# Input norm by token rows and side chunks ahead of main chunks, in a two-block transformer kernel on one core

## What is computed

```
def rms_norm(x, g):
    y = xf * lax.rsqrt(jnp.mean(xf * xf, axis=-1, keepdims=True) + RMS_EPS)
    return y * g

sh1, sc1, ga1, sh2, sc2, ga2 = split(silu(c) @ w_mod + b_mod)      # w_mod: 2048 x 12288; the same for c_ctx
px = (rms_norm(x,   norm_mix) * (1 + sc1)  + sh1)  @ w_in           # w_in: 2048 x 5568
pc = (rms_norm(ctx, norm_mix) * (1 + csc1) + csh1) @ w_in
```

## Time and profile before

| | us |
|---|---|
| median of 3 runs | 3162.58 |
| runs | 3152.15 to 3166.52 |
| the profiled execution, its own time | 3181.49 |
| its span in the profile | 3179.7 |
| TensorE busy | 3075.1 (97%) |
| VectorE busy | 2103.9 (66%) |
| ScalarE busy | 1571.3 (49%) |
| mean granted TensorE clock | 0.99 of full |

### The profile page before, as it was taken

How to read it: one execution, slowest core, us unless ns; L and a number is a source line. 1 busy time by engine, 2 the same in 40 slices (tenths; PEclk the granted TensorE clock), 3 DMA queues, 4 the chain that set the end, 5 groups by cost and what they waited for, 6 DMA issues and landing times.

```text
span 3179.7 us, 62622 instructions
## 1 busy us (share of the span) xinstructions
PE 3075.1 (97%) x26931; PEld 2652.4 (83%) x26931; DVE 2103.9 (66%) x2893; ACT 1571.3 (49%) x2161; POOL 245.3 (8%) x307
## 2 busy tenths in 40 slices
PE   6799999999999998999999999999999999999998
PEld 4578888888888887888888888888878888888887
DVE  5776656767787867555555556679977565655554
ACT  5555545565665644444444434456644444444333
POOL 1000000023332310000000000013200000000000
PEclk9899999999999999999999999999999999999999
DMA  9667766820000034666666565665555666666663
GB/s 334 202 212 244 244 221 212 256 79 8 12 8 8 8 110 152 198 186 186 185 186 186 184 194 185 207 181 157 157 164 173 186 186 187 187 188 193 186 186 126
DMA packets 549246, 529.56 MB, mean 167 GB/s; under 512 B 16916, under 2 KB 545706, under 8 KB 548074
## 3 DMA queue, kind: packets, MB, share of 16 engines
q1 hardware_dynamic: 546074, 516.08, 52.4%
q0 software_dynamic: 2832, 9.45, 0.9%
q10 hardware_dynamic: 64, 0.02, 0.0%
HBM read 521.28 MB, written 4.19 MB: 165 GB/s over the span
## 4 chain that ended last, share of the span: by engine, by line
PE 86%; DVE 9%; ACT 2%; DMA 2%; issue 1%; POOL 0%; DVEq 0%; ACTq 0%; POOLq 0%
PE ps L1991 38%; PE ps L1992 19%; PE ps L2122 10%; DVE lo L1210 3%; PE ps L2001 2%; PE ps L2030 2%; PE ps L2002 2%; PE ps L2003 2%; PE ps L2031 2%; PE ps L2384 1%; PE ps L2145 1%; PE ps L2132 1%; PE ps L2130 1%; ACT hi L796 1%; PE ps L2385 1%
## 5 line engine op out<-in xcount | busy, mean ns | idle before, releaser
L1210 DVE TENSOR_TENSOR lo<-raw,hi 128x1024 fp32r<-128x1024 f32 x936 | 1137.3, 1234 | 659.7 <-ACT hi L796 656.2
L796 ACT ACTIVATE hi<-raw 128x1024 fp32r<-128x1024 f32 x936 | 972.2, 1055 | 830.8 <-PE ps L1992 591.9
L1991 PE MATMUL ps<-mov,hi 128*128 128x512 f32 x3680 | 1303.8, 399 | 5.9 <-DVE mov L1272 4.6
L1992 PE MATMUL ps<-mov,lo 128*128 128x256 f32 x3680 | 1032.9, 281 | 0.0
L1991 PEld LDWEIGHTS ps<-mov,hi 128*128 128x128 f32 x3680 | 692.0, 188 | 180.9 <-issue 6.3
L1992 PEld LDWEIGHTS ps<-mov,lo 128*128 128x128 f32 x3680 | 695.5, 189 | 0.1
L1991 PE MATMUL ps<-hid,hi 128*128 128x512 f32 x704 | 248.8, 399 | 0.0
L2030 PE MATMUL ps<-hi,c 128*32 128x256 f32 x768 | 190.6, 288 | 40.5 <-DVE lo L1210 40.0
L816 ACT ACTIVATE tmp<-ps 128x512 f32<-128x512 f32 x157 | 93.8, 597 | 268.3 <-PE ps L1992 261.8
L1992 PE MATMUL ps<-hid,lo 128*128 128x256 f32 x704 | 197.7, 281 | 0.0
L2031 PE MATMUL ps<-lo,c 128*32 128x256 f32 x768 | 187.2, 284 | 0.0
(11 more groups left out here) (362 smaller groups left out, 4151.5 us busy)
## 6 DMA issues: line engine op xcount, KB each, us to landing
raw<-in_w_in SPq DMA_DIRECT2D x184, 512.0 KB, 4.6
raw<-in_w_mod SPq DMA_DIRECT2D x160, 512.0 KB, 4.9
raw<-in_w_gate SPq DMA_DIRECT2D x88, 512.0 KB, 4.6
raw<-in_w_up SPq DMA_DIRECT2D x88, 512.0 KB, 4.4
raw<-in_w_down SPq DMA_DIRECT2D x88, 512.0 KB, 4.3
raw<-in_w_ffn_gate SPq DMA_DIRECT2D x88, 512.0 KB, 4.6
raw<-in_w_ffn_up SPq DMA_DIRECT2D x88, 512.0 KB, 4.5
raw<-in_w_ffn_down SPq DMA_DIRECT2D x88, 512.0 KB, 4.4
```

Source lines behind the costliest of these rows:

```text
L796: act.activation(hi[:, s, :, :], src, ACT.Copy).then_inc(hi_ready, 1)
L1210: dve.tensor_tensor(lo[:, s, :, :], raw_at(ph, i, j)[0], hi[:, s, :, :].bitcast(F32), ALU.subtract)\
L1991: pe.matmul(ps[:, b, :], hi[:, s, kk, w], moving(k, None), start=first, stop=False)
L1992: mm = pe.matmul(ps[:, b, 0:T], lo[:, s, kk, w], moving(k, 0), start=False, stop=last)
```

## The change

1. **Squares by rows.** ScalarE squares each row tile of 128x2048 in one instruction that also sums along the row: two tiles of `ctx` after pair 4 and two of `x` after pair 5. The products with ones go. 1/rms is made of 128x4 numbers, after pairs 5 and 6 (`row_norm`), and VectorE writes `diag`, four 128x128 diagonals of these factors.
2. **Turn and scale in one product.** In pairs 7 to 14 TensorE multiplies blocks of the row tiles with `diag` (eight products of 128 columns per pair), which both turns and norms them. ScalarE copies the result out with the gain as scale (`scaled_at_pair`, four copies per pair, eight in pair 14). VectorE's 32 instructions of `first_product` go. The plain transposes of `x` stay (it is kept for the residual), four per pair in pairs 3 to 10, into bank 7, and VectorE copies both blocks at once; those of `ctx` go.
3. **The groups.** `first_hi` and `first_lo` no longer run two groups ahead of in_kv; all eight run in its first trip, at the chunks in `GROUP_AT`. TensorE waits once for all 32 scaled blocks before in_kv.
4. **The list of in_kv.** Each group of four side chunks now comes ahead of its main chunk, in every pair of every trip.

```diff
@@ -76,10 +76,9 @@
             self.order = [(False, p, c) for cs in ((0, 2, 3), (1,)) for p in range(pairs) for c in cs]
         for p in range(pairs if name not in ("out", "out_2") else 0):
             for c in self.rows_order:
-                self.order.append((False, p, c))
                 per = SIDES.get(name, 0) // pairs
-                if c < per:
-                    self.order += [(True, per * p + c, e) for e in range(n)]
+                group = [(True, per * p + c, e) for e in range(n if c < per else 0)]
+                self.order += group + [(False, p, c)] if name == "in_kv" else [(False, p, c)] + group
         self.chunks = len(self.order)
 
     def chunk(self, i, j):
...
@@ -324,14 +327,20 @@
 
     LOWS0 = PH["in_lora"].p0 + 1
 
-    XHAT_AT = {12: range(0, 8), 13: range(8, 16), 14: range(16, 24)}
-    XHAT_LATE = {3: range(24, 28), 7: range(28, 32)}
-    GROUP_AT = {1: 2, 2: 3, 5: 4, 6: 5, 8: 6, 9: 7}
+    NORM0 = 7
+    GROUP_AT = {0: 0, 1: 1, 2: 2, 3: 3, 6: 4, 8: 5, 10: 6, 12: 7}
+
+    def normed_at(p):
+        return range(2 * (p - NORM0), 2 * (p - NORM0) + 2) if NORM0 <= p < NORM0 + KB // 2 else range(0)
+
+    def scaled_at_pair(p):
+        return range(2 * (p - NORM0 - 1), 2 * (p - NORM0 - 1) + (4 if p == NORM0 + KB // 2 - 1 else 2)) if NORM0 < p < NORM0 + KB // 2 else range(0)
 
     def first_operand(n):
         q = 1 - n % 2
         k = n // 2
-        return q, k, (xhat[:, ds(k, 1), :], ctxT[:, ds(k, 1), :])[q]
+        x = xhat[:, k:k + 1, :] if k < KB - 4 else xhat_last[:, k - KB + 4:k - KB + 5, :]
+        return q, k, (x, ctxT[:, k:k + 1, :])[q]
 
     v_chain, a_chain, g_chain = sem("v_chain"), sem("a_chain"), sem("g_chain")
 
...
@@ -852,14 +862,23 @@
                 if p == VEC_AT:
                     act.wait_ge(vec_turned, 1)
                     act.activation(vec[:, :, :], ps[:, 5, :].rearrange("p (a n) -> p a n", a=4), ACT.Copy).then_inc(vec_ready, 1)
-                for k in turned_at(p):
-                    act.wait_ge(turned, k + 1)
-                    act.activation(ctxT[:, k, :], ps[:, TURN[k % 4], 0:T], ACT.Copy).then_inc(ctx_out, 1)
-                    if k >= 2:
-                        act.wait_ge(sq_used, k - 1)
-                    act.activation(sq[:, k % 2, :], ps[:, TURN[k % 4], :], ACT.Square).then_inc(sq_ready, 1)
-                if p == TURN0 + KB // 2 + 1:
-                    sqrt_of_variance(0, 2 * T)
+                if p in (TURN0 + 1, TURN0 + 2):
+                    act.wait_ge(row_in, 32)
+                    for h in range(2):
+                        src, n = ((crow, xrow)[p - TURN0 - 1], 2 * (p - TURN0 - 1) + h)
+                        if n:
+                            act.wait_ge(row_squared, n)
+                        act.activation(junk[:, :], src[:, h, :], ACT.Square, accum_out=row_sum[:, n:n + 1]).then_inc(row_squared, 1)
+                if p == TURN0 + 3:
+                    act.wait_ge(row_chain, 1)
+                    act.activation(row_root[:, :], row_var[:, :], ACT.Abs_reciprocal_sqrt).then_inc(row_rooted, 1)
+                for k in scaled_at_pair(p):
+                    if k == 0:
+                        act.wait_ge(gain_ready, 2)
+                    act.wait_ge(normed_turned, k + 1)
+                    for n in (2 * k, 2 * k + 1):
+                        q, _, dest = first_operand(n)
+                        act.activation(dest, ps[:, TURN[k % 4], (1 - q) * T:(2 - q) * T], ACT.Copy, scale=gain[:, q, k:k + 1]).then_inc(nt_ready, 1)
             gemm(PH["mod"], turn)
 
             def first_hi(g):
...
@@ -868,12 +887,12 @@
                     act.wait_ge(nt_ready, n + 1)
                     act.activation(mov1[:, ds(k, 1), 0, 1 - q, :], src, ACT.Identity, bias=modcol(0, q, k)).then_inc(nhi_ready, 1)
 
-            act.wait_ge(mod_ready, 4)
-            for g in range(2):
-                first_hi(g)
-
             def first_groups(i, j):
+                if i == 0 and j == 0:
+                    act.wait_ge(mod_ready, 4)
                 if i == 0 and j in GROUP_AT:
+                    if GROUP_AT[j] >= 6:
+                        act.wait_ge(mov_ready, 4 * GROUP_AT[j])
                     first_hi(GROUP_AT[j])
 
             def shift_both(i, p):
...
@@ -1280,16 +1299,32 @@
                 split(PH["mod"], 0, j)
 
 
+            def row_norm():
+                v, r, y = row_var[:, :], row_root[:, :], row_rstd[:, :]
+                dve.wait_ge(row_rooted, 1)
+                dve.tensor_tensor(v, v, r, ALU.mult).then_inc(row_chain, 1)
+                dve.wait_ge(row_chain, 2)
+                dve.scalar_tensor_tensor(out=v, in0=v, scalar=-0.5, in1=r, op0=ALU.mult, op1=ALU.mult).then_inc(row_chain, 1)
+                dve.wait_ge(row_chain, 3)
+                dve.scalar_tensor_tensor(out=y, in0=v, scalar=1.5, in1=r, op0=ALU.add, op1=ALU.mult).then_inc(row_chain, 1)
+                dve.wait_ge(row_chain, 4)
+                dve.tensor_tensor(diag[:, :, :], ident.rearrange("p (a n) -> p a n", a=1).broadcast_to([P, 4, P]),
+                                  y.rearrange("p (a n) -> p a n", n=1).broadcast_to([P, 4, P]), ALU.mult).then_inc(diag_ready, 1)
+
             def mod_row(i, p):
                 ph = PH["mod"]
                 part, n = 1 - p // 8, p % 8
                 dve.wait_ge(split_free, ph.last_chunk(i, p) + (1 + SPLIT_CREDIT))
                 dve.tensor_copy(mrow[:, n * CN:(n + 1) * CN], ps[0:4, ph.bank(p), 0:CN]).then_inc(bank_free, 1)
                 for k in turned_at(p):
-                    dve.wait_ge(sq_ready, k + 1)
-                    dve.tensor_copy(xT[:, k, :], ps[:, TURN[k % 4], T:2 * T]).then_inc(x_out, 1)
-                if p == TURN0 + KB // 2 + 1:
-                    variance(0, 2 * T)
+                    if k % 2 == 0:
+                        dve.wait_ge(turned, k // 2 + 1)
+                        dve.tensor_copy(xT[:, k:k + 2, :], ps[:, 7, :].rearrange("p (a t) -> p a t", a=2)).then_inc(x_out, 1)
+                if p == TURN0 + 2:
+                    dve.wait_ge(row_squared, 4)
+                    dve.tensor_scalar(row_var[:, :], row_sum[:, :], 1.0 / D, RMS_EPS, ALU.mult, ALU.add).then_inc(row_chain, 1)
+                if p == TURN0 + 3:
+                    row_norm()
                 if n == 7:
                     dve.wait_ge(vec_ready, 1)
                     dve.wait_ge(mcol_ready, p // 8 + 1)
...
@@ -1326,16 +1349,12 @@
                                              in1=mov1[:, ds(k, 1), 0, 1 - q, :].bitcast(F32), op0=ALU.add, op1=ALU.subtract).then_inc(mov_ready, 1)
 
             gemm(PH["mod"], mod_row)
-            dve.wait_ge(mod_ready, 4)
-            for g in range(2):
-                first_lo(g)
 
             def first_groups(i, j):
-                if i == 0:
-                    for item in XHAT_LATE.get(j, ()):
-                        first_product(item)
-                    if j in GROUP_AT:
-                        first_lo(GROUP_AT[j])
+                if i == 0 and j == 0:
+                    dve.wait_ge(mod_ready, 4)
+                if i == 0 and j in GROUP_AT:
+                    first_lo(GROUP_AT[j])
 
             def mod_row2(ph, i, m):
                 dve.wait_ge(split_free, ph.last_chunk(i, m, True) + (1 + SPLIT_CREDIT))
...
@@ -2039,19 +2058,22 @@
                     mm.then_inc(vec_turned, 1)
                 if p == TURN0:
                     pe.wait_ge(row_in, 32)
-                for k in range(2 * (p - TURN0), 2 * (p - TURN0) + 2):
-                    if k in turned_at(p):
-                        if k >= 4:
-                            pe.wait_ge(sq_ready, k - 3)
-                            pe.wait_ge(x_out, k - 3)
-                        for a, src in enumerate((crow, xrow)):
-                            for h in range(2):
-                                mm = pe.transpose(ps[:, TURN[k % 4], (2 * a + h) * P:(2 * a + h + 1) * P],
-                                                  src[:, h, k * P:(k + 1) * P], ident)
+                for k in turned_at(p):
+                    if k >= 2 and k % 2 == 0:
+                        pe.wait_ge(x_out, k // 2)
+                    for h in range(2):
+                        mm = pe.transpose(ps[:, 7, (2 * (k % 2) + h) * P:(2 * (k % 2) + h + 1) * P], xrow[:, h, k * P:(k + 1) * P], ident)
+                    if k % 2:
                         mm.then_inc(turned, 1)
-                    if 0 <= k - 2 < KB:
-                        pe.wait_ge(sq_ready, k - 1)
-                        pe.matmul(ps[:, 7, :], ones, sq[:, k % 2, :], start=(k == 2), stop=(k == KB + 1)).then_inc(sq_used, 1)
+                for k in normed_at(p):
+                    if k == 0:
+                        pe.wait_ge(diag_ready, 1)
+                    if k >= 4:
+                        pe.wait_ge(nt_ready, 2 * (k - 3))
+                    for n in range(4):
+                        mm = pe.matmul(ps[:, TURN[k % 4], n * P:(n + 1) * P], (crow, xrow)[n // 2][:, n % 2, k * P:(k + 1) * P], diag[:, n, :],
```

(23 more changed lines are left out.)

6 lines of the change are left out of this document (3 added, 3 removed).

## The result

The changed kernel takes 3183.9 us in the median of 7 runs (3168.2 to 3189.0), the kernel before, on the same chip, 3166.5 (3152.2 to 3180.5): a ratio of 1.0056 with a 95% interval of 1.003 to 1.0081. So the change makes the kernel slower by 0.6%, some 17 to 20 us: small, but both intervals leave out 1. Forecast were 3180 us and + 17 us.

The account below looks back on a forecast made before the run. TensorE, busy 97% of the span, was taken as the bound. From the profiled 3181.5 us, less 17.3 for the head start, plus 34.3 for seven pair ends, came 3198.5; against the median, 3180 us, range 3164 to 3194.

Parts of the forecast that it names:

- Part 1: Modulation stage up to pair 8: added squares open a 4.6 us gap; pair 8 ends at 88.2, 2.1 us behind.
- my bound of 4: Modulation stage up to pair 8: poor end of the range, 4 us behind; the good end was 2 ahead.
- Part 2: Modulation pairs 9 to 15: TensorE becomes the bound at 5.9 to 6.4 us a pair; in_kv's first chunk starts at 134.3.
- Part 3: First pair of in_kv: side chunks start at once; the pair ends at 176.2, 17.3 us ahead, bounds 11 to 23.
- the 1.7 us for the low clock: First pair of in_kv: the first main chunk runs partly at the low clock, adding 1.7 us.
- Part 4: Ends of in_kv pairs: TensorE waits 3.25 us for the third `lo`; 4.9 us lost at each of seven, 34.3 in sum.
- my 5.8 for a slow spell: In_kv pair ends: 5.8 us lost per end if the slow clock lasts as long as from 150.08, some 5 us.
- the rule of one price for all ends: In_kv pair ends: by the skill's HAM oscillation section all seven pay the low clock, 34.3 us in sum.
- none pays: In_kv pair ends: gap without slow clock, 26.8 us lost in sum, + 9.5, 3172 us; chance 24%.
- All three prices: Loss per in_kv pair end: 3.8 us without slow clock, 4.9 at half clock, 5.8 with a longer slow spell.
- The sum: Whole kernel: 17.3 us head start against 34.3 us lost gives + 17.0, 3180 us against the median.
- The likeliest case: Whole kernel: the forecast itself, head start outweighed by losses at in_kv pair ends, 3180 us; chance 50%.

Follow-up runs that it names:

- short squares: Changed kernel with the squares of the rows summed over 64 of 2048 elements, so not computing the function; 3171.3 us, ratio 1.0036 to the kernel before.
- second profile: Changed kernel run once more, unedited, for more executions beside the kernel before; 3187.2 us, ratio 1.0069 to the kernel before.
- norm-only run: Norm by rows put into the kernel before, with its old in_kv order and first two groups made ahead of in_kv; 3148.4 us, ratio 0.9956.
- order-only run: Kernel before, keeping its norm, with side chunks put ahead of main chunks in in_kv; 3190.7 us, ratio 1.0097.
- sides first in even pairs: Changed kernel with side chunks ahead of main chunks in even pairs alone, old order in odd pairs; 3162.1 us, ratio 0.9985 to the kernel before.
- short taps: Changed kernel with kv's outer taps on 8 of 256 tokens, so not computing the function; 3164.4 us, ratio 1.0008 to the kernel before.
- squares spread: Norm by rows with the old in_kv order and one square at chunks 15, 18, 21, 24 instead of two in a row; 3143.4 us, ratio 0.9950.

## Why the prediction was right, and where it was not

The time, 3180 against 3183.9, and the sign came out. By its steps:

- **Part 1, right as far as the splits, short by the clock.** The stations were met: the end of pair 5 at 60.8 (forecast 60.5), the last square done at 66.3 (66), the `lo` of chunk 26 at 68.6 (68), the gap 4.44 us (4.6). Then pair 6 ended at 72.19 instead of 70.3, since its last two chunks ran at half clock behind the gap, and the columns took 4.95 us instead of 3.75. Pair 8 ended at 90.87 instead of 88.2, 4.8 us behind the kernel before and so outside my bound of 4. (My own terms add up to 87.5: columns at 82.2 and 5.3 us for four chunks.) In the seven other profiles of the same code up to there it ended at 86.7 to 90.1, so 88.2 lies inside the scatter. What this part did not see is that the stage had more to give: the squares cost 6 to 10 us, and with short squares the new norm was 5 us ahead there, not 2 behind.
- **Part 2, right.** TensorE became the bound. Pairs 10 and 11 took 6.5 us against 6.4, pairs 12 to 14 6.15 against 5.9. The stage ended at 137.5 instead of 134.3: 2.7 us more from part 1, 1.0 more from these pairs, 0.5 less behind pair 14.
- **Part 3, right in the sum, wrong in what makes it.** 14.8 us ahead (16.7 in the second profile), against 17.3. From the columns to the pair's end it was 40.8 us against 41.9. But I had let the reader think that side chunks which "need no norm" bring a share. The norm-only run got 16.1 us without them. The terms were off as well: the first main product came 8.1 us behind the columns, not 7.2, and at full clock, so the 1.7 us for the low clock did not arise (in the second profile, at half clock until 145.5, the stretch took 42.8 us).
- **Part 4, right in its mechanism and nearly in its size.** The gap was 3.29 us against 3.25, and the third side chunk started 5.1 us after the end, as forecast. A pair cost 5.5 us on the mean against 4.9, seven of them 38.6 against 34.3, within the ends of 26.8 and 40.6. The missing part is the first 2.3 us of the main chunk at half clock: its rows took 0.63 us, 1.1 us more than I had counted. That was my 5.8 for a slow spell as long as at 150.08.
- **The clock.** Neither the rule of one price for all ends nor "none pays" holds. All three prices that I had laid out, 3.8, 4.9 and 5.8, occur, and the granted clock in the 4 us behind the gap tells them apart. The order-only run has an end with gap but without slow clock (230.82), where the pair took 39.0 us, that is 3.8 lost, the forecast's number to the tenth. TensorE's timeline there, and stretches behind this gap and behind the one that ends at 314.85 (start:end, length, TensorE busy, clock, DMA share, GB/s):

```profile
235.90 0.30 PE L2029 MATMUL ps<-hi,c 128*32 128x256 f32 x1 [3.29 <-DVE lo L1209]
...
236.00:240.00 4.00, 3.91 (x24) 1.00 0.67 215
...
316.00:320.00 4.00, 4.00 (x15) 0.57 0.92 273
```

  The gap is the 3.29 us of 223.53 above. The first row behind it does not tell the clock: it took 0.30 us at 314.85 too, and there the clock fell a little later and the pair took 40.2 us. Over four profiles (the changed kernel twice, order only, short squares) there are 28 ends with a gap of 3.2 to 3.3 us. At nine the clock stayed at 1.00, and five of these pairs took 39.0 us, the other four 39.3 to 39.9. At fourteen it was 0.58 to 0.70 on the mean, and the pairs took 39.8 to 40.3. At five, all in the changed kernel's first profile, it was 0.50, and the pairs took 41.0. Behind the three gaps of 2.6 us of the run with sides first in even pairs it fell twice, behind the seven of 1.7 us with short taps never. The Trainium skill, "TensorE: Matmul & The Clock Gate", section "HAM oscillation", has each round of such a loop pay. The changed kernel's first profile agrees at six of its seven ends (pairs of 40.2 to 41.0 us); at its last (423.41) and at that end of the order-only run the clock did not fall, and the measurement decides: such a loop may pay at some rounds and not at others. What decides it at a given end stays open.
- **The sum** was lucky in part: head start 2.5 us too large, loss 4.3 us too small, together 23.8 us instead of 17.0 by the first traces at the end of in_kv, but 17.4 by the medians. By the second trace of the changed kernel (head start 16.7, loss 31.2) it is 14.5: the forecast loss lies between the two profiles, the head start 0.6 us above the better of them. The likeliest case and the range, 3164 to 3194, held. That half of the change was good and half bad was in the parts, and the time alone would not have told it.

## What to carry to other kernels

Before moving short chunks to the front of a loop's round, ask what every feeding engine does at the round's end. If the split of chunk three stands behind an evacuation, the first two chunks must last as long as that evacuation, or the evacuation must move behind the splits. When a change has two independent halves, run each alone: here the halves were - 0.44% and + 0.97%, and the one that was worth keeping was hidden behind the other. Work put into a filler's slot should be priced on all engines: the side chunks that filled TensorE's wait delayed, on VectorE, the very operand that it waited for.

## What the runs showed of the hardware

The executions of one kernel come in steps. Of the 33 runs of before that stand beside the first four versions, 15 lie at 3148 to 3157 us, 15 at 3164 to 3172, and three at 3181 to 3184: steps of some 14 us. The traces place most of each step in the later stages, which no version touched. From the first product of in_lora's second pair to the start of the last copy into the output rows it was 2714 us in before's profile, 2699 and 2687 in the two of the changed kernel, and 2688 with the squares spread. Two stretches with the same products at the same granted clock, before and the norm alone (columns as above):

```profile
2500.00:2560.00 60.00, 60.00 (x342) 52.05 (x341) 36.41 (x38) 27.31 (x31) 0.00 (x0) 1.00 0.62 190
```

```profile
2500.00:2560.00 60.00, 60.00 (x348) 52.47 (x347) 37.58 (x39) 28.11 (x33) 0.00 (x0) 1.00 0.61 188
```

342 against 348 products in 60 us, without a gap in either: 2% in the pace of TensorE, which the granted clock does not show. Since some records can be missing from a trace, a landmark is the better witness. VectorE's last instruction of a round in this stage, the write of `hid_2a`, starts at 2483.80 and 2506.42 before, and at 2487.16 and 2509.34 with the norm alone. A round is 22.6 us in one and 22.2 in the other. Such rounds come in two stretches, near 1300 to 1750 us and 2430 to 2900 us. In the thirteen profiles each stretch has one of these two paces as the median of its 21 rounds: both fast in four, one of each in six, both slow in three (among these the kernel before). That gives three levels, as many as the steps, and some 9 us of each step. What sets the pace stays open. For the reading it means that two profiles are compared at landmarks close to the change, and not by their spans alone.

The same code also reached the end of pair 8 of the modulation stage at 86.7 to 90.9 us in eight profiles. From 79 to 86 us the granted clock was 1.00 in the four earliest (86.7 to 87.1) and 0.69 and 0.74 in the two latest (90.1 and 90.9).
